# An opening reordered: x's squares and half of the last modulation block on the matrix engine, the first weight remainder split later

## The chip, the core and the metric

The kernel runs on one core of one Trainium2 chip. The metric is the device time of one launch in microseconds (us); lower is better. Five engines work side by side: TensorE (PE, its weight loads shown as PEld), VectorE (DVE), ScalarE (ACT), GpSimd (POOL) and SyncE (SP), which here issues every load. They meet only through semaphores.

## The reference, cut to what matters

Two transformer blocks over 256 tokens of width 1024, in fp32. Only the start of the first bears on this case:

```
ada = c @ w_ada + b_ada                       # c: 1 x 1024, w_ada: 1024 x 6144
shift1, scale1, gate1, shift2, scale2, gate2 = split(ada, 6)
h = x * rsqrt(mean(x*x) + eps) * g_norm1 * (1 + scale1) + shift1
proj = h @ w_in                               # the first large product
```

So the first large product needs three things: the row sums of x's squares, and the first 2048 columns of `ada` (shift1 and scale1), each a dot product with all 1024 rows of `w_ada`. Everything after it (attention of two kinds, the MLP, the whole second block) is the same in both kernels.

## The kernel before, in words

All activations lie transposed: features on the partitions, tokens along the free axis. Large products are cut into 158 units (N_UNITS) of 1 MB of weights. A unit is loaded raw into one of four slots of `w_raw` (RING), then split in two parts of a reduced type: `w_hi` by a copy on ScalarE (`split_w` there, line 1243) and the remainder `w_lo = w_raw - w_hi` on VectorE (`split_w` there, line 1810). PE makes three products a unit: hi times hi, hi times lo, lo times hi (helper `mm`, line 514, which records every matrix instruction). A unit starts when its `w_lo` is done (`start_unit`). Each fp32 matmul shows as two records. Each engine's order is written out by hand; there is no scheduler.

The opening, until the first unit:

- SP issues, in this order: the small tables, 1 MB pieces a0 and a1 of `w_ada`, `consts`, `xT` (x), a2, a3, a4, a5, the first weight unit w0, a6, a7, w1, w2, w3 (`plan_loads`). Piece `a` holds half of the rows (four k-tiles of 128 x 512) of one block of 512 modulation columns: a0 and a1 are block 0, a6 and a7 are block 3, the last one of the opening.
- VectorE multiplies a piece's four k-tiles with c and adds them up in `ada_part` (its `ada_unit`, lines 1819 and 1821): a0, a1, a2, a4, a6, a7. After a2 it reads the mean square (line 1841), copies the `row` result (line 1962), does a4, normalizes x into `x_hat` (line 1967), splits w0 (`split_w(0)`), then does a6 and a7, adds the bias (line 1975), makes the gains (line 1977) and then h (line 1983).
- ScalarE squares x in one instruction into `qk` (line 1324), scales the four tiles of a3 (line 1329), splits w0 (line 1243), copies the 1 x 512 row of a5 out of PSUM (line 1333), then waits for the gains and makes `h_hi` (line 1337).
- GpSimd adds the squares of x in four instructions (`sum_squares("sum1")`, lines 1668 to 1671), takes the power -1/2 (line 1630), and adds a3's four tiles (lines 1685 and 1686).
- PE sums over partitions with a column of ones: `ada_block(j)` does this for block j, four matmuls of 128 x 128 with one moving column, and four more for each second operand (`other=`, another tile; `row=`, a 1 x 512 row). Its order: block 0, the sum of squares (`sum_x("sum1")`, two matmuls), the bias row product (`row`), the spread of the inverse root (`spread_sum`), `ada_rows(5)` (piece a5 as four matmuls with c as a one-column stationary operand and 512 moving columns), block 1, block 2 with a5's row, `keep_busy(WARM_A)` (five matmuls of 512 columns whose result nobody reads), block 3, `keep_busy(WARM_B)` (two of them), and then the first unit.

Loads that wait: w1 for a4 to be used (`ada_vector` 4), w2 for a5 (`ada_used` 1), w3 for a6 (`ada_vector` 5), w4 for the first `w_lo`.

Of the kernel before, what the change touches and what calls it, by code (L numbers as in the profile page):

```python
# [10 lines left out]
ACT = mybir.ActivationFunctionType  # L11
AX = mybir.AxisListType

P = 128
T = 256
TT = T // P
# [158 lines left out]
J_YM1, J_DIFF, J_MLP2 = 48, (49, 50, 51), 52  # L175

X_H4, X_H5, X_KV, X_MIX1, X_H7 = 0, 4, 8, 12, 16
SUMS = ("sum1", "sum3", "sum3g", "sum5", "sum6", "sum7")

G_FOX, G_DSA, G_M0, G_M1 = 0, 4, 8, 10  # L180

# [47 lines left out]
def two_blocks(nc, x, mem, w, vectors, tables, out):  # L229
# [34 lines left out]
    with ctx:  # L264
# [47 lines left out]
        def flat(t, a, b):  # L312

            return t[:, a:b, :].rearrange("p a n -> p (a n)")
# [1 line left out]
        ident, ones, heads2, causal = (consts[:, i * P:i * P + P] for i in range(4))  # L316

        sq_sum, row_inverse = ada_late, ada_late[:, 1, :]
        ada_row = fresh[0:1, 0, :]
        ada_home = {0: 0, 1: 0, 2: 1, 4: 0, 6: 1, 7: 1}  # L320
        h1_pairs = [fresh[:, 0, :], fresh[:, 1, :], probs[:, 0, :], probs[:, 1, :]]
        x_squares = [[probs[:, 0, :], probs[:, 1, :], probsT[:, 0, :], probsT[:, 1, :]],
# [114 lines left out]
        @block.sync  # L437
        def _(sp):
            def slot_view(n, at, width):
                slot = w_raw[:, slot_of[n], :]  # L440
                if units[n][0] == "N":
                    return slot.rearrange("p (k n) -> p k n", k=KT)[:, :, at:at + width]
                return slot.rearrange("p (k n) -> p k n", k=4)

            position = {what: i for i, what in enumerate(loads)}

            def load_unit(n):
                if n >= RING:
                    sp.wait_ge(lo_w, n - RING + 1)
                elif n == 1:  # L450
                    sp.wait_ge(ada_vector, 4)
                elif n == 2:
                    sp.wait_ge(ada_used, 1)
                elif n == 3:
                    sp.wait_ge(ada_vector, 5)
                for at, src in units[n][2]:
                    sp.dma_start(slot_view(n, at, src.shape[-1]), src).then_inc(raw_full[slot_of[n]], 16)

            def load_ada(a):
                if a == 7:  # L460
                    sp.wait_ge(ada_vector, 1)
                elif a in (8, 9):
                    sp.wait_ge(ada_vector, {8: 6, 9: 2}[a])
                elif a > 9:
                    sp.wait_ge(ada_part_sum, pool_turn(a - 2) + 1)
                rows = w["w_ada"].rearrange("(k p) n -> p k n", p=P)
                cols = rows[:, :, 256 * a:256 * a + 256]
                if a < ADA_FIRST:
                    cols = rows[:, 4 * (a % 2):4 * (a % 2) + 4, 512 * (a // 2):512 * (a // 2) + 512]
                sp.dma_start(ada_tiles(a), cols).then_inc(ada_first[a] if a < ADA_FIRST else ada_full[a % 2], 16)  # L470

            def load(first, last):

                for kind, n in loads[position[first]:position[last] + 1]:
                    (load_unit if kind == "w" else load_ada)(n)

            sp.dma_start(vec[:, :], tables["vec"]).then_inc(vec_in, 16)
            load(("a", 0), ("a", 1))
            sp.wait_ge(rel_set, 1)
            sp.dma_start(rel[0:32, :], vectors["rel_bias"].rearrange("(b h) -> b h", h=HEADS)).then_inc(small_in, 16)  # L480
            sp.dma_start(rel[64:64 + HEADS, 0:1], vectors["b_forget"].rearrange("(h o) -> h o", o=1)).then_inc(small_in, 16)
            sp.dma_start(buckets[0:33, :], tables["buckets"]).then_inc(small_in, 16)
            sp.dma_start(consts[:, :], tables["consts"]).then_inc(consts_in, 16)
            sp.dma_start(xT[:, :, :], x).then_inc(x_in, 16)
            load(("a", 2), ("w", 2))


            sp.wait_ge(misc_read, misc_no["row"] + 1)
            sp.dma_start(bias_dram, bias_row[0:HEADS, :]).then_inc(bias_out, 16)
            load(("w", 3), ("w", 4))  # L490
            sp.wait_ge(bias_out, 16)
            sp.wait_ge(ada_ready, 1)
            sp.dma_start(toeplitz, bass.AP(bias_dram.tensor, bias_dram.offset, [[1, P], [384, HEADS], [1, T]]))\
                .then_inc(bias_in, 16)
            load(loads[position["w", 4] + 1], ("w", N_GD))
            for half, tile in enumerate((mem_k, mem_v)):
                sp.dma_start(tile.rearrange("p l a t -> p (l a) t"), mem[:, 4 * half:4 * half + 4, :]).then_inc(mem_in[half], 16)
            load(loads[position["w", N_GD] + 1], ("w", N_M1V))
            sp.dma_start(flat(big, 6, 9)[:, 0:2 * T + P], tables["rope"]).then_inc(late_in, 16)
            sp.dma_start(big[:, 9, :], vectors["b_lam"].partition_broadcast(P)).then_inc(late_in, 16)  # L500
            sp.dma_start(chunk_mask, tables["chunks"]).then_inc(late_in, 16)
            load(("w", N_M1V + 1), ("w", N_UNITS - 1))
            for q in range(4):
                sp.wait_ge(xt_ready, 24 + q + 1)
                sp.dma_start(out[:, 2 * q:2 * q + 2, :], xT[:, 2 * q:2 * q + 2, :]).then_inc(y_out, 16)
            sp.wait_ge(y_out, 64)
# [3 lines left out]
        def _(pe):  # L510
# [99 lines left out]
            def keep_busy(times):  # L610

                for _ in range(times):
                    mm(acc[2][:, :], ident, consts[:, :], True, True)

            def ada_rows(a):

                tiles = ada_tiles(a)
                ada_in(pe, a)
                pe.wait_ge(vec_in, 16)
                for kt in range(4):  # L620
                    last = mm(acc[1][0:1, :], vec[:, V_C + 4 * (a % 2) + kt:V_C + 4 * (a % 2) + kt + 1],
                              tiles[:, kt, :], kt == 0, kt == 3)
                last.then_inc(ada_used, 1)

            def ada_block(j, part, other=None, row=None):
# [194 lines left out]
            pe.wait_ge(consts_in, 16)  # L820
            pe.wait_ge(ada_vector, 2)
            ada_block(0, ada_part[:, 0, :])
            sum_x("sum1")
            into_misc("row")
            pe.wait_ge(small_in, 48)
            mm(ps_misc[0:HEADS, 0:384], rel[0:33, :], buckets[0:33, :], True, True).then_inc(misc_full, 1)
# [4 lines left out]
            ada_block(1, ada_part[:, 1, :], other=probs[:, 0, :])  # L831
            pe.wait_ge(ada_vector, 4)
            pe.wait_ge(ada_copied, 1)
            ada_block(2, ada_part[:, 0, :], row=ada_row)
            keep_busy(WARM_A)
            pe.wait_ge(ada_vector, 6)
            ada_block(3, ada_part[:, 1, :])
            keep_busy(WARM_B)

            def first_unit():  # L840
# [382 lines left out]
        def _(act):  # L1223
# [57 lines left out]
            def squares_x(name):  # L1281

                i = SUMS.index(name)
                if i >= 3:
                    act.wait_ge(x_summed, i)
                for q in range(4):
                    if name == "sum3g":
                        for j in range(2):
                            k = 2 * q + j
                            last = act.activation(big[:, k, :], xT[:, k, :], ACT.Square, scale=vec[:, V_GF + k:V_GF + k + 1])  # L1290
                    else:
                        last = act.activation(x_squares[0][q], flat(xT, 2 * q, 2 * q + 2), ACT.Square)
                last.then_inc(x_squared, 1)
# [31 lines left out]
            for k in range(4):  # L1325
# [2 lines left out]
                    act.wait_ge(vec_in, 16)  # L1328
                last = act.activation(ada_tiles(3)[:, k, :], ada_tiles(3)[:, k, :], ACT.Copy, scale=vec[:, V_C + 4 + k:V_C + 5 + k])
            last.then_inc(ada_quarter_scaled, 1)  # L1330
            split_w(0)
            act.wait_ge(ada_used, 1)
            act.activation(ada_row, acc[1][0:1, :], ACT.Copy).then_inc(ada_copied, 1)
            act.wait_ge(ada_ready, 2)
            for q in range(4):
                for k in (2 * q, 2 * q + 1):
# [282 lines left out]
        def _(pool):  # L1619
# [40 lines left out]
            def sum_squares(name):  # L1660

                i = SUMS.index(name)
                squares = x_squares[name == "sum3g"] if i else [flat(qk, 2 * q, 2 * q + 2) for q in range(4)]
                pool.wait_ge(x_squared, i + 1)
                if i >= 3:
                    pool.wait_ge(misc_full, misc_no[SUMS[i - 1][:4]] + 1)
                for q in range(2):
                    last = pool.tensor_tensor(squares[q], squares[q], squares[2 + q], ALU.add)
                link(last)
                link(pool.tensor_tensor(squares[0], squares[0], squares[1], ALU.add))  # L1670
                pool.tensor_tensor(sq_sum[:, int(name == "sum3g"), :], squares[0][:, 0:T], squares[0][:, T:2 * T], ALU.add)\
                    .then_inc(x_summed, 1)
# [5 lines left out]

            pool.tensor_copy(head_bias[:, :, 0:P], ident[:, 64:64 + HEADS].unsqueeze(2).to_broadcast([P, HEADS, P]))\
                .then_inc(sel_ready, 1)  # L1680
            sum_squares("sum1")
            power("sum1")
            pool.wait_ge(ada_quarter_scaled, 1)
            quarter = ada_tiles(3)
# [113 lines left out]
        def _(dve):  # L1798
# [14 lines left out]
            def ada_unit(a):  # L1813

                tiles, part, k0 = ada_tiles(a), ada_part[:, ada_home[a], :], V_C + 4 * (a % 2)
                ada_in(dve, a)
                for k in range(4):
                    if k == 0 and a not in (1, 7):
                        last = dve.tensor_scalar(part, tiles[:, 0, :], vec[:, k0:k0 + 1], None, ALU.mult)
                    else:  # L1820
# [145 lines left out]
            dve.wait_ge(x_in, 16)  # L1966
            link(dve.tensor_tensor(x_hat[:, :, :], xT[:, :, :], acc[0][:, 0:T].unsqueeze(1).to_broadcast([P, KT, T]), ALU.mult))
            rstd_read()
            split_w(0)
            dve.wait_ge(ada_done, 2)  # L1970
            ada_unit(6)
            ada_unit(7)

            dve.wait_ge(ada_done, EARLY_COLUMNS)
            dve.tensor_tensor(ada[:, 0:16], ps_ada[:, 0:16], vec[:, V_ADA:V_ADA + 16], ALU.add).then_inc(ada_ready, 1)
# [532 lines left out]
```

## Time and profile before

| | us |
|---|---|
| median of 3 runs | 1091.81 |
| lowest, highest | 1090.96, 1093.19 |
| profiled execution, its own time | 1091.21 |
| its span in the trace | 1089.4 |
| PE busy | 1044.0 (96%) |
| VectorE busy | 646.1 (59%) |
| ScalarE busy | 541.9 (50%) |
| GpSimd busy | 372.8 (34%) |

The span runs from the first to the last instruction in the trace; the execution's own time holds what lies around it as well. PE's busy time has modelled ends, so it shows that PE is occupied, not that it works at its peak. Of the 45 us in which PE is not busy, 19 lie in the first 42 us, before the first unit: this is the stretch that the change touches.

### The profile page before, as it was taken

How to read it: one execution, taken by the hardware profiler on the slowest of the kernel's cores; microseconds unless marked ns; L12 is line 12 of the kernel's file. 1: busy time of each engine (PE TensorE's matmuls, PEld its weight loads, DVE VectorE, ACT ScalarE, POOL GpSimd, SP SyncE). 2: the span in 40 equal slices, each digit the busy share in tenths (PEclk: the TensorE clock that was granted, in tenths of full speed). 3: DMA queues.
4: the chain of work that ended last, by engine and by line, in shares of the span. 5: the costliest groups of instructions: out<-in, count | busy, mean ns of one | idle time of the engine just before them, and what ended most of it. 6: DMA issues, size and time to landing. Idle time of an engine off the chain costs nothing.

```text
span 1089.4 us, 19666 instructions
## 1 busy us (share of the span) xinstructions
PE 1044.0 (96%) x8492; PEld 1015.1 (93%) x8492; DVE 646.1 (59%) x824; ACT 541.9 (50%) x756; POOL 372.8 (34%) x196
## 2 busy tenths in 40 slices
PE   3999999998999999989999999999999989999998
PEld 1799999998999999989999999999988889999998
DVE  6968668666757454617855454444957666444443
ACT  2487777633665444544344444433664645444341
POOL 4028367231556242342111352222323212342231
PEclk9999999998999999999999999999999999999999
DMA  9988577445576655434355655556533145656541
GB/s 328 318 267 254 175 256 268 159 145 166 169 257 198 214 169 192 157 117 155 119 185 170 206 176 190 185 172 210 152 119 100 57 133 181 194 189 193 167 144 39
DMA packets 169859, 197.37 MB, mean 181 GB/s; under 512 B 5379, under 2 KB 137900, under 8 KB 169644
## 3 DMA queue, kind: packets, MB, share of 16 engines
q1 hardware_dynamic: 169772, 196.11, 55.5%
q8 instruction: 67, 1.10, 0.4%
q14 instruction: 20, 0.16, 0.0%
HBM read 195.03 MB, written 1.06 MB: 180 GB/s over the span
## 4 chain that ended last, share of the span: by engine, by line
PE 85%; DVE 7%; ACT 4%; issue 2%; DMA 1%; POOL 1%; DVEq 1%; SPq 0%; ACTq 0%; POOLq 0%
PE bank L514 83%; DVE w_lo L1810 3%; ACT w_hi L1243 1%; DMA xT<-in_x 1%; DVE v_tok L1821 1%; PE bank L784 1%; DMA ada_raw<-in_w_ada 0%; ACT h_hi L1337 0%; ACT h_hi L1278 0%; DVE big L2230 0%; DVE head_bias L2315 0%; ACT ada_raw L1233 0%; ACT big L1290 0%; DVE big L2218 0%; DVEq L2256 0%
## 5 line engine op out<-in xcount | busy, mean ns | idle before, releaser
L1810 DVE TENSOR_TENSOR w_lo<-w_raw,w_hi 128x2048 fp32r<-128x2048 f32 x158 | 388.9, 2465 | 246.9 <-ACT w_hi L1243 245.4
L514 PE MATMUL bank<-h_hi,w_hi 128*128 128x256 f32 x1328 | 374.4, 288 | 10.5 <-DVE w_lo L1810 4.9
L514 PE MATMUL bank<-h_hi,w_lo 128*128 128x256 f32 x1328 | 369.3, 285 | 0.0
L1243 ACT ACTIVATE w_hi<-w_raw 128x2048 fp32r<-128x2048 f32 x158 | 301.2, 1909 | 128.6 <-PE bank L514 121.5
L514 PE MATMUL bank<-h_lo,w_hi 128*128 128x256 f32 x1328 | 346.0, 283 | 0.0
L514 PE MATMUL bank<-u_hi,w_hi 128*128 128x256 f32 x1024 | 288.5, 285 | 4.2 <-DVE w_lo L1810 1.8
L514 PE MATMUL bank<-u_hi,w_lo 128*128 128x256 f32 x1024 | 286.4, 283 | 0.0
L1623 POOL TENSOR_TENSOR u_lo<-fresh,u_hi 128x512 fp32r<-128x512 f32 x60 | 142.3, 2373 | 404.6 <-ACT u_hi L1252 404.5
L514 PE MATMUL bank<-u_lo,w_hi 128*128 128x256 f32 x1024 | 277.2, 283 | 0.0
L514 PEld LDWEIGHTS bank<-h_hi,w_hi 128*128 128x128 f32 x1328 | 256.1, 194 | 16.5 <-DVE w_lo L1810 8.8
L514 PEld LDWEIGHTS bank<-h_hi,w_lo 128*128 128x128 f32 x1328 | 256.2, 194 | 0.0
L514 PEld LDWEIGHTS bank<-h_lo,w_hi 128*128 128x128 f32 x1328 | 242.0, 192 | 0.0
L514 PEld LDWEIGHTS bank<-u_hi,w_hi 128*128 128x128 f32 x1024 | 196.4, 192 | 5.6 <-DVE w_lo L1810 2.0
L514 PEld LDWEIGHTS bank<-u_hi,w_lo 128*128 128x128 f32 x1024 | 196.5, 192 | 0.0
L514 PEld LDWEIGHTS bank<-u_lo,w_hi 128*128 128x128 f32 x1024 | 191.0, 192 | 0.5 <-issue 0.5
L1437 ACT ACTIVATE fresh<-bank 128x512 f32<-128x512 f32 x48 | 28.6, 595 | 135.5 <-PE bank L514 135.5
L1655 POOL TENSOR_TENSOR ada_raw<-ada_raw 128x1024 f32<-128x1024 f32 (+1 forms) x32 | 80.8, 2526 | 40.3 <-ACT ada_raw L1233 39.0
L2133 DVE TENSOR_TENSOR fresh<-fresh 128x512 f32<-128x512 f32 x48 | 43.3, 903 | 75.9 <-ACT fresh L1437 75.8
L1233 ACT ACTIVATE ada_raw<-ada_raw,vec 128x256 f32<-128x256 f32 x128 | 52.8, 497 | 16.6 <-DMA ada_raw<-in_w_ada 16.6
L1252 ACT ACTIVATE u_hi<-fresh 128x512 fp32r<-128x512 f32 x60 | 37.4, 625 | 45.8 <-DVE fresh L1950 20.7
L1630 POOL TENSOR_TENSOR root<-root,minus_half 128x8 f32<-128x8 f32 (+2 forms) x15 | 30.9, 2061 | 69.7 <-DVE root L1841 40.1
L1658 POOL TENSOR_TENSOR ada_late<-ada_raw 128x256 f32<-128x256 f32 x16 | 23.9, 1492 | 39.7 <-PE bank L514 38.9
(253 smaller groups left out, 984.0 us busy)
## 6 DMA issues: line engine op xcount, KB each, us to landing
w_raw<-in_w_mlp SPq DMA_DIRECT2D x32, 1024.0 KB, 5.4
w_raw<-in_w_up SPq DMA_DIRECT2D x32, 1024.0 KB, 5.4
w_raw<-in_w_down SPq DMA_DIRECT2D x32, 1024.0 KB, 5.1
w_raw<-in_w_in SPq DMA_DIRECT2D x21, 1024.0 KB, 6.5
ada_raw<-in_w_ada SPq DMA_DIRECT2D x19, 1024.0 KB, 7.7
w_raw<-in_a_w_in SPq DMA_DIRECT2D x10, 1024.0 KB, 5.2
w_raw<-in_w_o SPq DMA_DIRECT2D x8, 1024.0 KB, 5.1
w_raw<-in_w_out SPq DMA_DIRECT2D x4, 1024.0 KB, 5.2
```

The costliest lines, as they stand in the source:

```text
L514: return pe.matmul(dst, lhsT, rhs, start=start, stop=stop, skip_group_check=True)
L784: last = pe.transpose(acc[2 + odd][:, c0:c0 + P], probs[:, odd, c0:c0 + P], ident)
L1233: last = act.activation(tiles[:, k, :], tiles[:, k, :], ACT.Copy, scale=vec[:, V_C + k:V_C + k + 1])
L1243: act.activation(w_hi[:, n % PARTS_RING, :], w_raw[:, slot_of[n], :], ACT.Copy).then_inc(hi_w, 1)
L1252: act.activation(flat(hi, tile, tile + 2), fresh[:, job % 2, :], ACT.Copy).then_inc(fresh_hi, 1)
L1437: act.activation(fresh[:, half, :], lin[lin_bank[n]][:, :], ACT.Relu).then_inc(evac_a, 1)
L1623: pool.tensor_tensor(flat(lo, tile, tile + 2), fresh[:, job % 2, :], flat(hi, tile, tile + 2).bitcast(F32), ALU.subtract).then_inc(fresh_l ...
L1630: pool.tensor_tensor(root[:, at:at + width], root[:, at:at + width], minus_half[:, 0:1].to_broadcast([P, width]), ALU.pow).then_inc(root_r ...
L1655: link(pool.tensor_tensor(tiles[:, 0:half, :], tiles[:, 0:half, :], tiles[:, half:2 * half, :], ALU.add))
L1658: pool.tensor_tensor(ada_late[:, turn % 2, :], tiles[:, 0, :], tiles[:, 1, :], ALU.add).then_inc(ada_part_sum, 1)
L1810: dve.tensor_tensor(w_lo[:, n % PARTS_RING, :], w_raw[:, slot_of[n], :], w_hi[:, n % PARTS_RING, :].bitcast(F32), ALU.subtract).then_inc(l ...
L2133: dve.tensor_tensor(fresh[:, half, :], fresh[:, half, :], fresh[:, half, :], ALU.mult)\
```

## The change

Four edits, all before the first unit:

1. `sum_squares("sum1")` on GpSimd is gone. PE sums the squares of x itself: 16 matmuls, each with a 128 x 128 tile of squares as stationary operand and one column of ones.
2. Of piece a7 VectorE multiplies two k-tiles instead of four. The other two go through PE as `ada_rows(7, first=2)`, behind `keep_busy(WARM_A)`; ScalarE copies the row out of PSUM, and block 3 takes it as `row=`, with four more matmuls.
3. VectorE's `split_w(0)` stands behind a7, and ahead of the wait for block 3.
4. ScalarE copies a5's row ahead of its `split_w(0)`, not behind it. Load a8 also waits for PE to have used a7.

The other lines only renumber the sums.

```diff
-        ada_row = fresh[0:1, 0, :]
+        ada_row = {5: fresh[0:1, 0, :], 7: fresh[0:1, 1, :]}
...
                     sp.wait_ge(ada_vector, {8: 6, 9: 2}[a])
+                    if a == 8:
+                        sp.wait_ge(ada_used, 2)
...
-            def ada_rows(a):
+            def ada_rows(a, first=0):
...
-                for kt in range(4):
+                for kt in range(first, 4):
                     last = mm(acc[1][0:1, :], vec[:, V_C + 4 * (a % 2) + kt:V_C + 4 * (a % 2) + kt + 1],
-                              tiles[:, kt, :], kt == 0, kt == 3)
+                              tiles[:, kt, :], kt == first, kt == 3)
...
             ada_block(0, ada_part[:, 0, :])
-            sum_x("sum1")
+            pe.wait_ge(x_squared, 1)
+            for k in range(KT):
+                for tt in range(TT):
+                    last = mm(ps_misc[:, tt:tt + 1], qk[:, k, tt * P:tt * P + P], ones[:, 0:1], k == 0 and tt == 0, k == KT - 1)
+            last.then_inc(misc_full, 1)
             into_misc("row")
...
-            ada_block(2, ada_part[:, 0, :], row=ada_row)
+            ada_block(2, ada_part[:, 0, :], row=ada_row[5])
             keep_busy(WARM_A)
+            ada_rows(7, first=2)
             pe.wait_ge(ada_vector, 6)
-            ada_block(3, ada_part[:, 1, :])
+            pe.wait_ge(ada_copied, 2)
+            ada_block(3, ada_part[:, 1, :], row=ada_row[7])
             keep_busy(WARM_B)
...
+            act.wait_ge(ada_used, 1)
+            act.activation(ada_row[5], acc[1][0:1, :], ACT.Copy).then_inc(ada_copied, 1)
             split_w(0)
-            act.wait_ge(ada_used, 1)
-            act.activation(ada_row, acc[1][0:1, :], ACT.Copy).then_inc(ada_copied, 1)
+            act.wait_ge(ada_used, 2)
+            act.activation(ada_row[7], acc[1][0:1, :], ACT.Copy).then_inc(ada_copied, 1)
...
-            sum_squares("sum1")
             power("sum1")
...
-                for k in range(4):
+                for k in range(2 if a == 7 else 4):
...
-            split_w(0)
             dve.wait_ge(ada_done, 2)
             ada_unit(6)
             ada_unit(7)
+            split_w(0)
```

## Rows read from the trace of the kernel before

**Rows 1.** The page: engines' busy time, and the chain that ended last, by engine.

```profile
PE 1044.0 (96%) x8492; PEld 1015.1 (93%) x8492; DVE 646.1 (59%) x824; ACT 541.9 (50%) x756; POOL 372.8 (34%) x196
...
PE 85%; DVE 7%; ACT 4%; issue 2%; DMA 1%; POOL 1%; DVEq 1%; SPq 0%; ACTq 0%; POOLq 0%
```

**Rows 2.** Chain of waits, 0 to 75 us: start us, us, what.

```profile
4.00 8.81 DMA xT<-in_x
12.82 0.02 issue
12.84 1.92 ACT qk L1324
14.76 0.07 issue
14.83 2.67 POOL qk L1668 x2
...
20.34 1.03 PE bank L514 x4
...
38.36 0.75 DVE v_tok L1821
39.11 0.04 DVEq L1825
39.15 0.04 issue
39.19 1.07 PE bank L514 x8
```

**Rows 3.** Timeline, PE: start us, us, engine, line, operation.

```profile
13.77 1.84 PE L514 MATMUL bank<-consts,v_tok 128*128 128x1 f32 x8 [13.77 <-DVEq L1825]
...
21.61 1.44 PE L514 MATMUL bank<-probsT,rel 33*8 33x384 f32 x2 [0.25 <-DVE root L1841]
...
24.13 4.40 PE L514 MATMUL bank<-w_raw,vec 128*1 128x512 f32 x8
```

**Rows 4.** Timeline, weight loads of the 512-column matmuls of `ada_rows(5)`.

```profile
24.94 0.13 PEld L514 LDWEIGHTS bank<-w_raw,vec 128*1 128x1 f32 x1 [0.72 <-issue]
25.79 0.09 PEld L514 LDWEIGHTS bank<-w_raw,vec 128*1 128x1 f32 x1 [0.73 <-issue]
26.22 0.08 PEld L514 LDWEIGHTS bank<-w_raw,vec 128*1 128x1 f32 x1 [0.34 <-issue]
```

**Rows 5.** Timeline, PE, blocks 1 and 2, first and last pairs, then keep_busy.

```profile
28.46 0.38 PE L514 MATMUL bank<-consts,v_tok 128*128 128x1 f32 x2
...
30.05 0.36 PE L514 MATMUL bank<-consts,probs 128*128 128x1 f32 x2
...
30.44 0.35 PE L514 MATMUL bank<-consts,v_tok 128*128 128x1 f32 x2
...
32.58 0.58 PE L514 MATMUL bank<-consts,fresh 1*128 1x1 f32 x2
...
33.09 6.00 PE L514 MATMUL bank<-consts 128*128 128x512 f32 x10
```

**Rows 6.** Windows, PE: stretch, busy (records), granted clock, DMA share, GB/s.

```profile
33.00:34.00 1.00, 1.00 (x2) 0.50 1.10 350
...
36.00:37.00 1.00, 1.00 (x4) 0.99 1.11 350
```

**Rows 7.** Timeline, the other engines: a5's row copy, a3's sum, x_hat, a7.

```profile
29.72 0.57 ACT L1333 ACTIVATE fresh<-bank 1x512 f32<-1x512 f32 x1
...
24.74 1.33 POOL L1686 TENSOR_TENSOR probs<-big 128x512 f32<-128x512 f32 x1
...
28.38 2.29 DVE L1967 TENSOR_TENSOR qk<-xT,bank 128x2048 f32<-128x2048 f32 x1 [0.18 <-issue]
...
36.00 3.11 DVE L1821 SCALAR_TENSOR_TENSOR v_tok<-ada_raw,vec,v_tok 128x512 f32<-128x512 f32 x4
```

**Rows 8.** DMA issue of a7, and its median time to landing.

```profile
24.81 0.87 SPq L470 DMA_DIRECT2D ada_raw<-in_w_ada  x1
...
ada_raw<-in_w_ada SPq DMA_DIRECT2D x1, 1024.0 KB, 8.6
```

**Rows 9.** Windows of all engines, a later stretch of low clock: PE, PEld, DVE, ACT, POOL.

```profile
264.70:268.10 3.40, 2.54 (x12) 2.57 (x13) 3.33 (x8) 1.26 (x2) 1.45 (x2) 0.50 0.26 102
```

More of the change, by code:

```diff
@@ L177 @@
 X_H4, X_H5, X_KV, X_MIX1, X_H7 = 0, 4, 8, 12, 16
-SUMS = ("sum1", "sum3", "sum3g", "sum5", "sum6", "sum7")
+SUMS = ("sum3", "sum3g", "sum5", "sum6", "sum7")
 G_FOX, G_DSA, G_M0, G_M1 = 0, 4, 8, 10
@@ L1283, in squares_x @@
                 i = SUMS.index(name)
-                if i >= 3:
+                if i >= 2:
                     act.wait_ge(x_summed, i)
@@ L1662, in sum_squares @@
                 i = SUMS.index(name)
-                squares = x_squares[name == "sum3g"] if i else [flat(qk, 2 * q, 2 * q + 2) for q in range(4)]
-                pool.wait_ge(x_squared, i + 1)
-                if i >= 3:
+                squares = x_squares[name == "sum3g"]
+                pool.wait_ge(x_squared, i + 2)
+                if i >= 2:
                     pool.wait_ge(misc_full, misc_no[SUMS[i - 1][:4]] + 1)
```

## The prediction

> **What bounds the kernel now.** I read the page first. PE is busy for 96% of the span and holds 85% of the chain that ended last [rows 1], so a change in the opening is worth what it moves the first large product, and nothing behind that product takes the shift back: the chain goes on through waits between engines and through loads that are themselves issued on such waits. Second view, the chain of waits of the first 75 us [rows 2]: x lands at 12.8, ScalarE squares it until 14.8, GpSimd adds the squares until 20.3, PE sums them until 21.4; later it is VectorE's last multiply of a7 (ends 39.11), then block 3 on PE (39.19 to 40.26), then the gains and h. The reader is to see that the GpSimd and VectorE work which the change takes away stands in this chain. Third view, PE's timeline beside it [rows 3, 5]: the chain names only what came last. `keep_busy(WARM_A)` is 10 records from 33.09 to 39.09, so PE itself is free only 0.1 to 0.2 us before VectorE is done with a7. PE is a second chain, as long as the first. What the change puts on PE ahead of block 3 is not hidden.
>
> **Edit 1, the squares on PE.** Removed: GpSimd's four adds (14.83 to 20.30) and PE's two matmuls (until 21.37) [rows 2]. Added: 16 matmuls, 32 records, with one moving column. Block 0 is the same form: 8 records in 1.84 us, the last of which takes about 0.35, so one every 0.21 us [rows 3]. They start behind block 0, at 15.5, when the squares have been there since 14.8, and end at 15.5 + 31 x 0.213 + 0.35 = 22.5. That is 1.1 us later than before: term **+1.1**. The burst replaces 5.5 us of GpSimd by 7 us of PE. Bounds: the same form at the higher clock comes every 0.11 us (28.46 to 30.05 is seven pairs in 1.59 us [rows 5]), which would end it at 19.2, 2.2 us early. I take the low-clock price, since the nearest row, block 0 just ahead of it, has it. The granted clock column says 1.00 there, but the durations do not: the 512-column records of `ada_rows(5)` come 0.85 us apart until 25.79 and 0.43 apart from then on [rows 4], the two levels 1.2 and 2.4 GHz.
>
> Does the burst itself raise the clock? The row: blocks 1 and 2 are such one-column records for 4.6 us without a pause, and in their last stretch the pair takes 0.5 instead of 0.31; the granted clock is then 0.50 at 33, and it is back to 0.99 at 36 to 37 only with the 512-column records of `keep_busy` before it [rows 5, 6]. So one-column work doesn't hold the clock up, and I don't expect it to raise it. The Trainium skill ("TensorE: Matmul & The Clock Gate", Part 1) has the full clock follow a sustained busy stretch, and gives no exception for such matmuls. By that rule the burst would turn fast part way; the first rival below works out, from rows, what that would give.
>
> Behind the sum everything in order moves by +1.1: the mean square, the `row` product (1.44 [rows 3]), the power, the spread, `ada_rows(5)`, which starts at 25.2. The clock rose at 25.8, so it has one slow record ahead of that and not two: **-0.4**. It ends near 29.1. GpSimd's power comes first, then a3's sum (before: done at 26.07 [rows 7]), now near 27.0, still ahead of block 1. VectorE is idle from 18.4 (a2 is no longer slowed by GpSimd) until the sum is there: no gain, because a4 stands behind the mean square in its order. `x_hat` ends near 31.7 (before: 30.67 [rows 7]).
>
> **Edit 4, a5's row.** The copy took 0.57 and started at 29.72, behind ScalarE's split of w0 [rows 7]; block 2 stood still from 30.25 to 30.44 for it. That wait goes: **-0.2**. ScalarE's split of w0 then ends near 31.6 and is covered: VectorE comes to it only at 36.
>
> **Edit 3, the split of w0 on VectorE (2.3 us).** It leaves VectorE's chain ahead of a6. a6 starts at 31.8, a7 at 34.7; a7 landed at 24.81 + 8.6 = 33.4 [rows 8], so it is no bound. Two tiles of 0.76 instead of four end at 36.3, against 39.11 before: VectorE is 2.8 us earlier. The split then runs from 36.4 to 38.7, under PE's work. If PE were free it would cost up to 2.3 in front of the bias add. The load w4 waits for it and goes out 2 us later, for a unit that starts over 15 us later: nothing. Queued behind the new wait of load a8 are only w7 and later ones, far off.
>
> **Edit 2, half of a7 on PE.** Ahead of block 3, behind `keep_busy`: 4 records of 512 columns at 0.43 = **+1.7** (at 1.2 GHz 3.4). Then PE waits for ScalarE: the last record's completion 0.2, copy 0.57, handing on twice 0.05 = **+0.8** (bounds 0.7 and 1.0; nothing is queued on PE that could fill it). Block 3 has 16 records instead of 8. Block 2 has the same form: seven pairs from 30.44 to 32.58, so 0.31 a pair and 2.5 for eight, with completion 2.6, against 1.07 [rows 2, 5]: **+1.5**. The slack of PE against VectorE goes: **-0.2**.
>
> **`keep_busy(WARM_A)`** cost 6.0 in the trace, 4.3 if all ten records were at 2.4 GHz. It starts near 34.6 now; if the clock falls and rises at about the same times, more of block 2 lies in the low stretch (four pairs at 0.5, +0.8) and less of `keep_busy` (1.4 us instead of 2.9, -0.75). I take **0**. Bounds: no fall at all -1.7; a low stretch once more as long +1.7.
>
> **Sum:** 1.1 - 0.4 - 0.2 + 1.7 + 0.8 + 1.5 - 0.2 + 0 = +4.3. Block 3 ends near 44.6 instead of 40.26, and h, the split of w1 and the second unit follow as before. GpSimd's missing 5.5 us and VectorE's missing 2.8 end in waits. Against the profiled execution: 1091.21 + 4.3 = 1095.5. The median of the runs is 0.6 above it. The case's own range is +2.6 to +6.2, 1093.8 to 1097.4.
>
> **Rivals.**
> A, the burst turns fast and one-column work keeps the clock up. For it: it is busy without a gap from 13.8. Against it: rows 5 and 6. Half of the burst at each level ends it at 20.9, `ada_rows(5)` is all fast and ends near 27.2, block 2 at 31.6, `keep_busy` takes 4.3 and ends at 35.9, rows of a7 at 37.6, the copy at 38.4, block 3 at 41.0: +0.7, 1091.9. So even a fast PE takes up VectorE's gain and is not faster.
> B, the clock is low at a7's rows, block 3 and `keep_busy(WARM_B)`: two thin stretches (the wait for ScalarE, 2.5 us of one-column work) lie there. Price: 1.7 for the rows, 1.5 for block 3 (pairs of 0.5), up to 1.7 for WARM_B, of 4.3 + 4.9 = +9.2, 1100.4. It decides if the fall comes before 42.
> C, low stretches elsewhere. At 264.7 to 268.1 PE has 2.54 us of work at clock 0.50 [rows 9]; three such stretches follow one another there, 7.1 us of PE work, so up to 3.6 us hang on where they fall. A shift of 4.3 us moves it all. If it is shed: +0.7, 1091.9; if it is added, 1099.
> D, the other side: VectorE's chain is the end after all, because `keep_busy` ends by 34.6. Then block 3 starts at 36.4, takes 2.6, VectorE's split is in front of the bias add only until 38.7, h starts at 39.3 instead of 40.7: -1.4 and with a5's row earlier up to -2.5, 1088.7. It decides from a `keep_busy` under 1 us behind a block 2 that ends at 33.9; ten records at the higher level take 4.3, which speaks against it.
>
> **How the numbers follow.** Chances: forecast 0.60, A 0.13, B 0.07, C 0.12 (two thirds of it shed), D 0.08. The time is the forecast's, 1095.5. For 8 in 10 the range goes down into A and C and up part of the way to B: 1091.6 to 1098.6. A difference of 0.2%, 2.2 us, is what a measurement of this kernel can tell from none. Faster by more: D, 0.08. Within: A and the shed part of C, 0.21. Slower: forecast, B, the rest of C, 0.71.
>
> **What would show it.** The sum of squares on PE: 32 records over about 7 us, mean square read at 22.5 (A: before 21). a7's rows starting later than VectorE's end of a7, block 3 starting from ScalarE's copy and not from VectorE: `ada` add at 44 to 45. VectorE's split of w0 ended well before it. If the add comes before 41, PE was not the bound and I am wrong; if it comes at 44 and the time is not up by 3 to 5 us, something behind the opening gives it back.

## The result, and the profile after

| | before | after |
|---|---|---|
| median of 5 runs, us | 1091.81 (1090.96 to 1093.19) | 1100.94 (1097.77 to 1101.23) |
| profiled execution, its own time | 1091.21 | 1100.94 |
| span in the trace | 1089.4 | 1099.2 |
| ratio after/before, 95% interval | | 1.0068 (1.0054 to 1.0083) |

The change makes the kernel slower by 0.68%, some 7.4 us (5.9 to 9.1 by the interval); the two medians stand 9.1 us apart and the two profiled executions 9.8 us of span. Forecast was slower by 4.3 us. PE is busier by 14 us and GpSimd less busy by 5 [rows 1]:

```profile
PE 1058.4 (96%) x8532; PEld 1026.0 (93%) x8532; DVE 642.0 (58%) x822; ACT 542.5 (49%) x757; POOL 368.1 (33%) x192
```

The chain of waits of the kernel after, first 85 us (start us, us, what), against [rows 2]. From 13.7 on it is PE alone, but for the mean square and ScalarE's row copy. GpSimd and VectorE's a7 are gone from it, as the change intended, and PE has taken their place:

```profile
13.69 8.68 PE bank L516 x40
22.37 0.02 issue
22.40 0.17 DVE root L1850
22.57 0.04 issue
22.61 19.87 PE bank L516 x60
42.48 0.02 issue
42.51 0.59 ACT fresh L1343
43.10 0.14 issue
43.24 19.09 PE bank L516 x116
```

Its timeline, against [rows 3, 5, 7]: the squares' burst, a5's rows, VectorE's half of a7 and its split of w0, then PE's filler, a7's rows, the first and last pair of block 3 and the bias add. VectorE is done at 39.1; the add waits 7.02 us more for PE.

```profile
15.39 6.96 PE L516 MATMUL bank<-consts,qk 128*128 128x1 f32 x32
...
25.14 5.08 PE L516 MATMUL bank<-w_raw,vec 128*1 128x512 f32 x8
...
34.41 6.25 PE L516 MATMUL bank<-consts 128*128 128x512 f32 x10
...
35.11 1.54 DVE L1830 SCALAR_TENSOR_TENSOR v_tok<-ada_raw,vec,v_tok 128x512 f32<-128x512 f32 x2
...
36.79 2.29 DVE L1819 TENSOR_TENSOR w_lo<-w_raw,w_hi 128x2048 fp32r<-128x2048 f32 x1
...
40.59 1.88 PE L516 MATMUL bank<-ada_raw,vec 128*1 128x512 f32 x4
...
43.24 0.35 PE L516 MATMUL bank<-consts,v_tok 128*128 128x1 f32 x2 [0.77 <-ACT fresh L1343]
...
45.48 0.58 PE L516 MATMUL bank<-consts,fresh 1*128 1x1 f32 x2
45.99 3.78 PE L516 MATMUL bank<-consts 128*128 128x512 f32 x4
46.10 0.17 DVE L1984 TENSOR_TENSOR ada<-bank,vec 128x16 f32<-128x16 f32 x1 [7.02 <-PE bank L516]
```

And the windows view of the same kernel: stretch, its length, busy time (records) of PE, PEld, VectorE, ScalarE, GpSimd, granted clock, DMA share, GB/s. Between 45.2 and 52.0 the granted clock is 0.50, over the end of block 3, `keep_busy(WARM_B)` and the first unit. The kernel before has nothing like it there: its only stretch of 0.50 in the opening is 32.6 to 36.0, over the end of block 2 and the filler, which the changed kernel has too (35.0 to 38.4).

```profile
38.40:45.20 6.80, 6.03 (x23) 2.87 (x22) 0.68 (x1) 0.59 (x1) 0.00 (x0) 1.00 0.95 302
45.20:52.00 6.80, 6.80 (x20) 4.71 (x21) 5.83 (x12) 5.49 (x9) 2.56 (x2) 0.50 0.49 156
52.00:56.40 4.40, 4.40 (x38) 4.40 (x38) 4.32 (x3) 2.16 (x2) 0.00 (x0) 1.00 0.12 17
```

### The profile page after: what moved, and what is told of

It reads as the page before. It is cut to its first block, busy times and chain, and to the rows that moved or that the text cites. A ratio compares the mean times of both kernels' runs of the same rounds, so it can differ in the third digit from the quotient of the medians.

```text
span 1099.2 us, 19744 instructions
## 1 busy us (share of the span) xinstructions
PE 1058.4 (96%) x8532; PEld 1026.0 (93%) x8532; DVE 642.0 (58%) x822; ACT 542.5 (49%) x757; POOL 368.1 (33%) x192
## 4 chain that ended last, share of the span: by engine, by line
PE 84%; DVE 7%; ACT 4%; DMA 2%; issue 2%; DVEq 1%; POOL 0%; SPq 0%; ACTq 0%; POOLq 0%
PE bank L516 82%; DVE w_lo L1819 3%; DMA ada_raw<-in_w_ada 2%; ACT w_hi L1251 2%; ACT ada_raw L1241 1%; PE bank L786 0%; DVE fresh L1870 0%; DVE v_tok L1830 0%; ACT h_hi L1286 0%; DVE big L2239 0%; DVE head_bias L2324 0%; DVE fresh L1864 0%; ACT big L1298 0%; DVE big L2227 0%; DVEq L2265 0%
## 5 line engine op out<-in xcount | busy, mean ns | idle before, releaser
L2142 DVE TENSOR_TENSOR fresh<-fresh 128x512 f32<-128x512 f32 x48 | 43.3, 901 | 75.0 <-ACT fresh L1447 74.9
```

The source lines that it names most:

```text
L2142: dve.tensor_tensor(fresh[:, half, :], fresh[:, half, :], fresh[:, half, :], ALU.mult)\
```

## The experiments

Ratios are against the kernel before on the same chip, with 95% intervals; 0.001 is 1.1 us. A difference between two experiments compares two such ratios, often from two chips, so it is uncertain by 2 us or more. In each trace two marks are read: when the bias add starts (its block 3 is done), and when the second unit starts.

**The parts one by one.** `e1_squares_only` is edit 1 alone:

```diff
-            sum_x("sum1")
+            pe.wait_ge(x_squared, 1)
+            for k in range(KT): ...   # 16 matmuls of squares with a column of ones
...
-            sum_squares("sum1")
```

> Edit 1 alone: PE sums the squares in 32 one-column records; the rest is as before. Theory T (PE is a second chain as long as VectorE's, and everything put ahead of block 3 on it counts): +1.1 us for the later sum, x_hat and block 2 1.0 later, block 3 ends near 41.3, in all +0.7 to +1.5 (1092.5 to 1093.3); and no second stretch of low clock behind block 3, since there is no wait and no long one-column work there. Rival K (the later clock stretches move with any shift, whatever is edited): +3 or more.

Measured: 1.0020 (1.0010 to 1.0029), +2.2 us. The sum is done as late as expected (mean square at 22.0), but the add starts at 43.29. a5's rows, a term that I had made smaller, took 5.93 us and not 4.40 [rows 3], blocks 1 and 2 behind them 5.55 and not 4.63, and the filler started at 36.15. The windows view (columns as above) has the low clock over them for 6.8 us, where the kernel before has it for 3.4:

```profile
24.75 5.93 PE L514 MATMUL bank<-w_raw,vec 128*1 128x512 f32 x8
...
36.15 6.31 PE L514 MATMUL bank<-consts 128*128 128x512 f32 x10
...
32.90:39.70 6.80, 6.80 (x18) 4.66 (x18) 6.45 (x9) 0.00 (x0) 0.00 (x0) 0.50 1.08 341
```

No low clock lies behind block 3.

`e2_half_only` is edit 2 alone (a7's second half through PE, its row copied, block 3 with the row).

```diff
             keep_busy(WARM_A)
+            ada_rows(7, first=2)
             pe.wait_ge(ada_vector, 6)
-            ada_block(3, ada_part[:, 1, :])
+            pe.wait_ge(ada_copied, 2)
+            ada_block(3, ada_part[:, 1, :], row=ada_row[7])
```

> Edit 2 alone: half of a7 through PE behind keep_busy, with ScalarE's row copy. VectorE still splits w0 ahead of a6. Theory T: +1.7 for the four records, +0.8 for the wait for the copy, +1.5 for block 3 with the row, -0.2 slack: +3.8 until block 3's end (near 44.1), and on top 2 to 4 us where the granted clock is 0.50 at keep_busy(WARM_B) and in the first unit: 1095.5 to 1099.5. Rival V (VectorE's chain ends last, PE's filler gives way): half of a7 is 1.5 us less on VectorE, so -1 to 0.

Measured: 1.0058 (1.0043 to 1.0073), +6.3 us: the main part of the loss. The add starts at 44.74, 0.6 behind the 44.1 of theory T, and from 43.3 the clock is 0.50 for 6.8 us. Windows of PE alone (length, busy (records), granted clock, DMA share, GB/s):

```profile
43.00:44.00 1.00, 1.00 (x6) 0.65 1.09 346
...
46.00:47.00 1.00, 1.00 (x2) 0.50 0.87 160
...
51.00:52.00 1.00, 1.00 (x11) 1.00 0.00 0
```

`e3_order_only` is edits 3 and 4 alone.

```diff
+            act.wait_ge(ada_used, 1)
+            act.activation(ada_row, acc[1][0:1, :], ACT.Copy).then_inc(ada_copied, 1)
             split_w(0)
...
-            split_w(0)
             dve.wait_ge(ada_done, 2)
             ada_unit(6)
             ada_unit(7)
+            split_w(0)
```

> Edits 3 and 4 alone: VectorE splits w0 behind a7, ScalarE copies a5's row ahead of its split. VectorE is done with a7 2.3 us earlier (36.8). Theory T: PE is in keep_busy until 38.9, so block 3 starts 0.2 to 0.4 earlier and no more: 1091.2 to 1091.8, no difference. Rival V: the 2.3 us come off in full, near 1089.5.

Measured: 1.0005 (0.9995 to 1.0015), no difference. VectorE's a7 ends at 37.85, PE's filler runs from 35.40 for 6.23 us, and the add waits for PE:

```profile
34.74 3.11 DVE L1821 SCALAR_TENSOR_TENSOR v_tok<-ada_raw,vec,v_tok 128x512 f32<-128x512 f32 x4
35.40 6.23 PE L514 MATMUL bank<-consts 128*128 128x512 f32 x10
...
42.45 0.17 DVE L1975 TENSOR_TENSOR ada<-bank,vec 128x16 f32<-128x16 f32 x1 [2.19 <-PE bank L514]
```

`e4_no_half` is the changed kernel with edit 2 undone.

> The changed kernel without edit 2 (a7 wholly on VectorE): squares on PE, w0 split late, a5's row copied early. Theory T: +1.1 - 0.4 (row copy, slack) = +0.7, 1092.0 to 1092.8, so edit 2 is all but 1 us of the loss. Rival K (the squares' burst leaves the clock low and that costs most of the loss): +4 or more, with low clock at keep_busy(WARM_B).

Measured: 1.0021 (1.0011 to 1.0031), +2.3 us, the same as edit 1 alone. 2.2 + 6.3 + 0.5 is 9.0, and the three together cost 7.4 (5.9 to 9.1): the parts add up within their intervals.

**Is PE the chain ahead of block 3?** `e6_short_filler` changes the length of the filler in the changed kernel.

```diff
-WARM_A, WARM_B = 5, 2
+WARM_A, WARM_B = 2, 2
```

> The changed kernel with keep_busy(WARM_A) of 2 matmuls instead of 5. Theory T (PE is what block 3 waits for): six records less, 2.6 us at 2.4 GHz and up to 5.1 at 1.2, so block 3 ends that much earlier, 1096 to 1098.5. Rival V (VectorE or the copy is last): nothing. Rival F (the filler pays for itself, since with less of it the clock stays low through a7's rows and block 3): half or more of the gain is lost, 1099 or above.

Measured: 1.0039 (1.0025 to 1.0052), 3.1 us less than the changed kernel for six records, with intervals that lie just apart. `e10_before_filler10` lengthens the filler of the kernel before (`WARM_A = 10`):

> The kernel before with keep_busy(WARM_A) of 10 matmuls instead of 5: ten records more in front of block 3. Theory T (PE's order is a chain as long as VectorE's): +4.3 us at 2.4 GHz less 0.2 of slack, 1096.5 to 1097. Rival V (PE has room there): +2 or less.

Measured: 1.0050 (1.0035 to 1.0065), +5.5 us. `e11_before_filler3` shortens it (`WARM_A = 3`):

> The kernel before with keep_busy(WARM_A) of 3 matmuls. VectorE's a7 ends at 39.1 whatever PE does. Theory T with both chains about equal: at the times of the profile no gain; in executions where the clock rises late (PE is then up to 2 us behind VectorE) up to 2 come off, so 0 to -1 on average, 1091.6 to 1092.6. Rival F (the filler holds the clock up for the first units): +1 or more.

Measured: 0.9991 (0.9982 to 1.0000), -1.0 us, at the edge of the noise. PE's order bounds the opening of the changed kernel. Before, more on PE costs nearly its whole length and less on PE gains little: block 3 then starts from VectorE's a7, and the two chains are about equally long.

**The wait for the copy and the clock.** `e5_fill_gap`:

```diff
             ada_rows(7, first=2)
+            keep_busy(1)
             pe.wait_ge(ada_vector, 6)
```

> The changed kernel with one more filler matmul (2 records of 512 columns, 0.43 us each) between a7's rows and block 3, where PE stood for 0.8 us waiting for ScalarE's copy. Theory G (the low clock behind block 3, 45.2 to 52.0, comes of that wait and the one-column block 3 together): block 3 starts within 0.2 us of before, the low stretch goes or is halved, 2 to 3.5 us come off: 1097.5 to 1099. Rival O (block 3's one-column work alone does it, the wait doesn't matter): no change, 1100.5 to 1101.5.

Measured: 1.0071 (1.0056 to 1.0086), nothing gained. Its trace shows no low clock behind block 3, and the filler in the gap cost only 0.1 us (a7's rows to block 3 took 2.77 and not 2.65). But the low clock is not less in all: ahead of block 3 it lasts 6.8 us (33.0 to 39.8) where the changed kernel has 3.4, and one stretch of 3.4 at 903.4 is new. Over the whole kernel, the last 3 us aside, the stretches of 0.50 add up to 27.3 us in both. Theory G's gain did not come. `e7_rows_first`:

```diff
-            keep_busy(WARM_A)
             ada_rows(7, first=2)
+            keep_busy(WARM_A)
```

> The changed kernel with a7's rows ahead of keep_busy(WARM_A) and not behind it, so that the filler covers ScalarE's copy and block 3 follows dense work without a wait. Theory G: 0.8 us of waiting off, and the low stretch behind block 3 gone: 1096.5 to 1098. Rival O: only the 0.8 us, 1100 to 1100.5.

Measured: 1.0046 (1.0030 to 1.0062), 2.4 us less, with intervals that overlap, but a low stretch of 3.4 us stands at 45.9: the wait isn't needed for it. `e9_no_row`:

```diff
-            pe.wait_ge(ada_copied, 2)
-            ada_block(3, ada_part[:, 1, :], row=ada_row[7])
+            ada_block(3, ada_part[:, 1, :])
...
+            dve.wait_ge(ada_copied, 2)      # VectorE, ahead of h
```

> The changed kernel, but block 3 takes neither the row (four matmuls less) nor the wait for ScalarE's copy; a7's rows and the copy still run, their half of a7 is left out of the sum. Theory S+C (the loss of edit 2 is structure, 1.7 rows + 0.8 wait + 1.5 row matmuls, and on top about 2 us of low clock that the thin stretch of wait and one-column work brings): 2.3 of structure and 2 of clock come off, 1100.5 - 4.3 = 1096.2. Rival S (structure only, the clock is the rows' or the shift's own): -2.3, 1098.2.

Measured: 1.0040 (1.0026 to 1.0054), 3.0 us less: between the two, and its trace has no low clock behind block 3. VectorE's added wait cost nothing, since the copy ended at 44.92 and the add started at 45.31. Not decisive by time alone, and the trace is one draw: here too the low stretch ahead of block 3 is 6.8 long.

**How often?** The changed kernel and edit 2 alone were each profiled twice more.

> The changed kernel again, one profiled execution, for its clock. Theory C (the stretch behind block 3 belongs to edit 2): low clock between 43 and 53 again, in at least three of the four new executions. Rival P (it is a matter of where an execution falls): in one of four or none.

> As r_after_1, a second execution. Where the stretch is missing, block 3's end to the second unit takes 8.7 us as in the kernel before, where it is there about 10.3.

> Edit 2 alone again, one profiled execution. Theory C: low clock between 42 and 51. The clock's first rise stays at 26 to 28.7 as in every trace without edit 1; with edit 1 it was at 28.2 to 29.7.

> As r_half_1, a second execution: low clock between 42 and 51 by theory C, none by rival P.

All four had it. Their times are 1102.28 and 1100.04 us for the changed kernel, 1100.40 and 1099.10 for edit 2 alone, and 1095.81 for one execution of the kernel before beside them. Read from the timelines and windows of all traces (us):

| kernel | bias add | second unit | between | low clock behind block 3 |
|---|---|---|---|---|
| changed, three executions | 46.10, 48.28, 46.40 | 56.40, 58.25, 55.54 | 10.30, 9.97, 9.14 | 6.8, 6.8, 3.4 |
| edit 2 alone, three | 44.74, 44.85, 44.98 | 54.81, 54.00, 55.03 | 10.07, 9.15, 10.05 | 6.8, 3.4, 6.8 |
| e7, rows ahead of the filler | 44.91 | 53.95 | 9.04 | 3.4 |
| before, filler of 3 (e11) | 40.04 | 49.08 | 9.04 | 3.4 |
| edit 4, filler of 3 (e13, below) | 41.32 | 50.39 | 9.07 | 3.4 |
| before | 40.28 | 48.93 | 8.65 | none |
| e1, e3, e4, e5, e6, e9, e10, and e8, e12, e14 (below) | 39.30 to 47.67 | 47.94 to 56.32 | 8.64 to 8.65 | none |

Six of six executions of the changed kernel and of edit 2 alone have the stretch, and it costs 0.5 us where it is 3.4 long and 1.3 to 1.65 where it is 6.8. PE loses more than that: in the kernel before it stood still for 1.00 us ahead of the second unit, waiting for VectorE's split of w1, and the slower work fills this wait. One of the second executions, windows of all engines, and that wait in the kernel before:

```profile
46.70:53.50 6.80, 6.80 (x19) 4.69 (x20) 5.15 (x11) 4.81 (x9) 2.57 (x2) 0.50 0.49 154
...
48.93 0.39 PE L514 MATMUL bank<-h_hi,w_hi 128*128 128x256 f32 x1 [1.00 <-DVE w_lo L1810]
```

Which part of edit 2 brings the stretch isn't shown. The single traces of e5, e6 and e9 have none, and e6 only shortens the filler. In all three the low stretch ahead of block 3 is 6.8 long; but so it is in one execution of the changed kernel (33.0 to 39.8), which has the stretch behind block 3 as well.

**Versions meant to beat both.** `e8_rows_first_short`: squares on GpSimd, edits 2 to 4, a7's rows ahead of a filler of 2.

> A version meant to beat both: the squares stay on GpSimd as before, edits 2, 3 and 4 are in, a7's rows stand ahead of the filler, and the filler has 2 matmuls. Block 2 ends at 33.0, a7's rows 33.5 to 35.2 (36.9 if slow), filler 1.7 to 3.4, VectorE is done with its half of a7 at 36.5 and with w0's split at 38.8, block 3 takes 2.6. Theory T: block 3 ends between 39.5 and 42, against 40.3: -0.8 to +1.7, 1091.7 to 1094.2 by this chip's median of before near 1092.5. Rival F (too little dense work ahead of the first unit, clock low there): 1095 or above.

Measured: 1.0016 (1.0005 to 1.0027). `e12_row_early` has the squares on GpSimd and edits 2 to 4, and issues the four row matmuls before VectorE is done:

```diff
-            keep_busy(WARM_A)
+            ada_rows(7, first=2)
+            keep_busy(1)
+            pe.wait_ge(ada_copied, 2)
+            for c in range(4):
+                mm(ps_ada[:, 12 + c:13 + c], ada_row[7][:, c * P:c * P + P], ones[0:1, 0:1], True, False)
+            keep_busy(1)
             pe.wait_ge(ada_vector, 6)
             ada_block(3, ada_part[:, 1, :])   # its matmuls add to the sums that are open
```

> A version meant to beat both: squares on GpSimd, edits 3 and 4, a7's rows ahead of the filler, one filler matmul over ScalarE's copy, then the four row matmuls (they open the sums), one filler matmul, and behind VectorE's half of a7 only block 3's own four. Theory S: against e8_rows_first_short the 1.5 us of row matmuls leave the end of the chain where PE waits for VectorE, and where PE is late (clock low until 39) nothing: 1093 to 1094, 0.5 to 1.5 below it, still not below the kernel before by more than 0.2%. Rival: with less filler the clock is low at the first units, 1095 or above.

Measured: 1.0004 (0.9992 to 1.0017). As written each of the four opens its sum anew, and the result lacks a part of the sums; that it is the row's part of some columns is inferred from the code, not shown. The instructions are the ones that a correct version would need. `e13_copy_filler3` is edit 4 with a filler of 3, `e14_order_filler2` edits 3 and 4 with a filler of 2 and the squares and a7 left as before.

> The kernel before with edit 4 (a5's row copied ahead of ScalarE's split) and keep_busy(WARM_A) of 3 matmuls. VectorE's a7 ends at 39.1 and is last. Theory T: as with the short filler alone, 0.5 to 1.3 us below the kernel before. Rival F (early copy or short filler leave the clock low): no gain or a loss.

> The kernel before with edits 3 and 4 and keep_busy(WARM_A) of 2 matmuls: VectorE's a7 ends at 36.8, PE's filler at 35 to 38.7, block 3 at 38 to 39.8; but VectorE splits w0 from 36.9 to 39.2 to 40.1 in front of the bias add. Theory T: add at 39.3 to 40.3, so 1 to 2 us below the kernel before and up to 1 below e13. Rival F: low clock behind block 3 gives 1 to 2 back.

Measured: e13 1.0010 (1.0000 to 1.0020), no gain: ScalarE's early copy delays its split of w0, VectorE waits 1.25 us for that, and a low stretch of 3.4 lies behind block 3. e14 0.9988 (0.9978 to 0.9997), 1091.53 us against 1091.94: the one version whose interval lies below the kernel before, by 0.12%, under what a single measurement would tell. Its timeline shows edit 3 at work once the filler is out of its way. The add is no longer PE's to delay, but VectorE's split of w0 stands in front of it until 39.3:

```profile
32.85 3.67 PE L514 MATMUL bank<-consts 128*128 128x512 f32 x4
33.85 3.12 DVE L1821 SCALAR_TENSOR_TENSOR v_tok<-ada_raw,vec,v_tok 128x512 f32<-128x512 f32 x4
37.09 2.29 DVE L1810 TENSOR_TENSOR w_lo<-w_raw,w_hi 128x2048 fp32r<-128x2048 f32 x1
37.97 1.96 PE L514 MATMUL bank<-consts 128*128 128x512 f32 x4
39.30 0.17 DVE L1975 TENSOR_TENSOR ada<-bank,vec 128x16 f32<-128x16 f32 x1
```

## Why the prediction was right and wrong

The direction and the mechanism were right: PE's written order is a second chain as long as VectorE's, and the change loads it. The size was off, by the terms of TensorE's clock: +4.3 forecast, +7.4 (5.9 to 9.1) measured, and 1100.94 lies outside the range. Term by term, profiled execution after against before, until the bias add:

| step | forecast | measured | from |
|---|---|---|---|
| squares' burst | +1.1 | +1.0 | mean square at 22.40 and 21.40 |
| `ada_rows(5)` | -0.4 | +0.7 | 5.08 and 4.40 |
| blocks 1 and 2, a5's wait gone | -0.2 | -0.4 | 4.27 and 4.63 |
| filler, with PE's slack | 0 - 0.2 | +0.1 | 6.18 and 6.10 |
| a7's rows and the copy | +2.5 | +2.65 | 40.59 to 43.24 |
| block 3 with the row | +1.5 | +1.8 | 2.86 and 1.09 |
| sum | +4.3 | +5.8 | add at 46.10 and 40.28 |
| add to second unit | 0 | +1.65 | 10.30 and 8.65 |
| behind the second unit | 0 | +2.3 | 1042.8 and 1040.5 |

**What held.** One-column matmuls cost what block 0 said: 32 records in 6.96 us against 6.95 worked out. VectorE's gain was there (2.8 forecast; a7 ended at 36.65 against 39.11) and came to nothing. The half of a7 on PE cost its three terms. Edit 3 alone gave nothing, and e10, e6 and e14 show why: the filler is in its way. Rival D falls with that: a shorter VectorE chain moved the end only where the filler was cut too. Rival A falls too: the burst stayed slow throughout. Rival C, the later low stretches, is not decided (below).

**What failed is the clock, in two steps.** The first is the clock's rise: "it has one slow record ahead of that and not two: -0.4", and "I take **0**" for the low stretch over blocks 1 and 2 and the filler. I kept the time of the rise fixed at 25.8. In the nine traces with edit 1 the records turn fast at 28.1 to 29.7, in the eleven without it at 25.8 to 28.6. `ada_rows(5)` took 5.08 to 6.03 us with edit 1 (mean 5.75) and 4.40 to 5.92 without it (mean 5.11), the kernel before being the lowest of all twenty. That term is +0.6, not -0.4. Blocks 1 and 2 behind it take 5.5 to 5.7 us where the low stretch over them is 6.8 long, against 4.3 to 4.6 where it is 3.4. It was 6.8 long in six of the nine traces with edit 1 and in two of the eleven without (e3, e8), so the mean rises by another 0.6, where I had 0. With 0.9 for the later sum (means 22.1 and 21.2) this makes 2.2, and edit 1 alone measured +2.2. The profiled execution of the changed kernel happened to have the short stretch, so the table above doesn't show the second 0.6. Why the rise comes 2.2 us later on average, for rows that start 0.9 later, isn't shown. Rows 4 showed one execution's rise, and I read it as the kernel's.

The second is rival B, low clock at a7's rows, block 3 and `keep_busy(WARM_B)`, at 0.07 and with nothing for it in the sum. It came in six of six executions, but only from the end of block 3 on: a7's rows and most of block 3 still ran at 2.4 GHz. So its price of 4.9 was too high. Measured are 1.1 us as the mean of the six behind the add, since 1.00 of PE's loss there filled a wait, plus 0.3 to 0.6 in block 3 itself where the fall is early (four of the six, 0.3 as the mean of all). These 1.4 and the 1.5 by which edit 1 outran its +0.7 (1.1 - 0.4) are 2.9 of the 3.1 us that the forecast lacked. Having read in rows 5 and 6 that the clock fell over one-column work, I should have given that stretch a share of the forecast.

By the Trainium skill ("TensorE: Matmul & The Clock Gate", Part 1) a sustained busy stretch brings the full clock. Here 8.7 us of unbroken one-column matmuls (13.69 to 22.37) did not; the measurement decides. The same section calls the moment of the transition variable from run to run, and on that the traces agree: the eleven just named differ by 1.5 us in one group of eight records.

**What stays open.** Behind the second unit the changed kernel's three executions take 1042.2 to 1042.8, the kernel before 1040.5, but e1, e3, e4 and e10, where nothing behind the opening differs either, 1041.4 to 1042.9. So most of the 2.3 can be that the profiled execution of before was a good one, and not the change; this is an argument and not shown (on the later chips its median was 1091.9 to 1093.4). Whether a shift of the opening moves the later low stretches to a worse place on average is not settled: of the six executions of the changed kernel and of edit 2 alone, five had two stretches near 490 and 500 us; of before, e1, e3, e4 and e10 only e3 had two. In e9 there were two as well. Nor is it settled why the filler in the gap (e5) and the missing row (e9) gave back less time than their traces without the stretch suggest; both have one trace each, and the low stretches ahead of block 3 and behind the opening differ from trace to trace.

## What to carry to other kernels

When an engine's order is written by hand, the engine that a chain names last is not the only bound: look where every other engine's queue stands at that moment, and count filler work as work. Moving a reduction to TensorE as one-column matmuls with a new stationary tile each pays a whole weight load for a column (32 loads fill 6.95 of the burst's 6.96 us), here at the low clock, and the burst didn't bring the clock up. A time of a clock change read from one execution is a draw: price it from both levels, and give a thin stretch ahead of dense work its cost.

## What the runs showed of the hardware that was not expected

- The clock fell at the end of block 3 or behind it in all six executions of the changed kernel and of edit 2 alone, and with a filler of 3 instead of 5 also without edit 2 (e11, e13), where `keep_busy` had cost 4.54 us and not 6.00. With still less filler it did not (e6, e8, e12, e14, one trace each), so these runs don't show that the filler protects the first unit. In e11 the low stretch cost 0.4 us (9.04 against 8.65), and the add came only 0.24 earlier, since VectorE's a7 is there the last.
- An fp32 matmul with one moving column (two records) comes every 0.31 us where full stationary tiles alternate with one-row tiles, and every 0.22 where all are full, at the same clock of 1.00 (block 3 after, and [rows 5]): mixing in the smaller operand makes it slower. Which part waits isn't shown.
- With GpSimd silent, VectorE did a2 in 0.49 + 2.33 us, against 0.81 + 4.44 beside GpSimd's adds. The parts alone say the same: 0.48 + 2.33 in e1, 0.83 + 4.43 in e2. The 2.4 us went into VectorE's wait for the sum (4.10 us before the mean square):

```profile
15.97 2.33 DVE L1830 SCALAR_TENSOR_TENSOR v_tok<-big,vec,v_tok 128x512 f32<-128x512 f32 x3
...
22.40 0.16 DVE L1850 TENSOR_SCALAR root<-bank 128x2 f32<-128x2 f32 x1 [4.10 <-PE bank L516]
```
